# GpSimd's first subtraction behind each norm waits for the diagonal matrices, and TensorE multiplies a block of ones meanwhile

## The reference, cut to what matters

```python
def rmsnorm(x, w):
    x32 = x.astype(jnp.float32)
    y = x32 * lax.rsqrt(jnp.mean(x32 * x32, axis=-1, keepdims=True) + NORM_EPS)
    return (y * w.astype(jnp.float32)).astype(x.dtype)
...
    for i in range(DEPTH):
        h = rmsnorm(x, norm_mix[i])
        x = x + token_mixer(h, w_in[i], ...)
        x = x + peer(rmsnorm(x, norm_ffn[i]), peer_wq[i], peer_keys[i], peer_u[i], peer_v[i])
    return rmsnorm(x, norm_final)
```

## Time and profile before

| | us |
|---|---|
| median of 3 runs | 2109.36 |
| lowest and highest | 2107.76 and 2110.62 |
| the profiled execution, its own time | 2112.14 |
| span of its trace, first to last instruction | 2110.0 |
| granted TensorE clock, mean over the span | 0.984 |

### The profile page before, as it was taken

One profiled execution on the slowest core, in us unless ns is written; L12 is line 12 of the kernel. 1 busy time (PEld: TensorE's weight loads), 2 busy tenths in 40 slices (PEclk: granted clock), 3 DMA queues, 4 the chain that ended last, 5 costly groups with the idle time before them and its releaser, 6 DMA issues.

```text
span 2110.0 us, 40295 instructions
## 1 busy us (share of the span) xinstructions
PE 2021.6 (96%) x13604; PEld 1856.2 (88%) x13604; DVE 1258.7 (60%) x2835; ACT 973.1 (46%) x1431; POOL 1283.8 (61%) x624
## 2 busy tenths in 40 slices
PE   7988999999999999999989879999999999999998
PEld 7787999999999888888787869999999998888886
DVE  6555099538888544444475550994388885444444
ACT  4444454653333454554544434446533334445454
POOL 5334679976666555555463337899766665555553
PEclk9999999999999999999999999999999999999999
DMA  6423455554444555555534225545444445555554
GB/s 208 145 80 100 160 185 167 171 175 140 139 139 139 169 190 196 190 195 193 184 121 151 90 81 174 195 159 175 166 140 140 138 140 176 194 194 191 196 190 139
DMA packets 93242, 338.44 MB, mean 160 GB/s; under 512 B 10353, under 2 KB 10737, under 8 KB 93169
## 3 DMA queue, kind: packets, MB, share of 16 engines
q1 hardware_dynamic: 93168, 337.53, 47.7%
HBM read 336.44 MB, written 1.05 MB: 160 GB/s over the span
## 4 chain that ended last, share of the span: by engine, by line
PE 85%; DVE 7%; POOL 3%; issue 2%; ACT 1%; DMA 1%; POOLq 0%; DVEq 0%; SPq 0%; ACTq 0%
PE PS L885 33%; PE PS L829 10%; PE PS L824 10%; PE PS L825 10%; PE PS L837 5%; PE PS L530 4%; POOL WL L444 3%; DVE G L1382 2%; PE PS L514 2%; PE PS L515 2%; PE PS L750 2%; PE PS L519 2%; PE PS L496 1%; PE PS L625 1%; DVE G L1379 1%
## 5 line engine op out<-in xcount | busy, mean ns | idle before, releaser
L444 POOL TENSOR_TENSOR WL<-ring,WH 128x1024 fp32r<-128x1024 f32 x360 | 910.0, 2533 | 486.1 <-ACT WH L955 244.6
L1119 ACT CAST WH<-ring 128x1024 fp32r<-128x1024 f32 x512 | 538.0, 1051 | 814.1 <-PE PS L825 380.8
L470 POOL TENSOR_TENSOR HL<-G,HH 128x256 fp32r<-128x256 f32 x256 | 372.5, 1455 | 324.4 <-ACT HH L1212 324.3
L1702 DVE TENSOR_TENSOR WL<-ring,WH 128x1024 fp32r<-128x1024 f32 x248 | 303.7, 1225 | 371.0 <-ACT WH L1119 371.0
L824 PE MATMUL PS<-HH,WH 128*128 128x256 f32 x2048 | 512.2, 288 | 0.0
L825 PE MATMUL PS<-HL,WH 128*128 128x256 f32 x2048 | 501.3, 283 | 0.0
L825 PEld LDWEIGHTS PS<-HL,WH 128*128 128x128 f32 x2048 | 392.2, 192 | 0.0
L824 PEld LDWEIGHTS PS<-HH,WH 128*128 128x128 f32 x2048 | 391.8, 191 | 0.0
L885 PE MATMUL PS<-WH,HH 128*128 128x512 f32 x1024 | 315.4, 389 | 3.0 <-issue 3.0
L885 PE MATMUL PS<-WH,HL 128*128 128x512 f32 x1024 | 315.3, 389 | 0.0
L829 PE MATMUL PS<-HH,WL 128*128 128x256 f32 x2048 | 289.1, 284 | 12.4 <-POOL WL L444 12.4
(11 more groups left out here) (237 smaller groups left out, 2306.8 us busy)
## 6 DMA issues: line engine op xcount, KB each, us to landing
ring<-stream SPq DMA_DIRECT2D x636, 512.0 KB, 3.3
X<-x_t SPq DMA_DIRECT2D x4, 256.0 KB, 4.4
out_t<-X SPq DMA_DIRECT2D x2, 512.0 KB, 2.7
CN<-consts SPq DMA_DIRECT2D x1, 843.5 KB, 9.7
WF<-last SPq DMA_DIRECT2D x1, 512.0 KB, 10.2
PR<-params SPq DMA_DIRECT2D x2, 239.0 KB, 4.4
CN<-consts SPq DMA_DIRECT2D x1, 64.0 KB, 5.1
```

The lines of the kernel that those rows point to most:

```text
L444: nc.gpsimd.tensor_tensor(WL[:, b, :], ring[:, slot, :], WH[:, b, :].bitcast(F32), ALU.subtract).then_inc(done, 1)
L470: nc.gpsimd.tensor_tensor(GL[:, s, :], G[:, tile, :], GH[:, s, :].bitcast(F32), ALU.subtract).then_inc(L.gl_ready, 1)
L1119: nc.scalar.copy(WH[:, b, :], ring[:, slot, :]).then_inc(L.hi_ready, 1)
L1702: V.tensor_tensor(WL[:, s % 2, :], ring[:, (U0 + s) % SLOTS, :], WH[:, s % 2, :].bitcast(F32), ALU.subtract).then_inc(L.vlo_ready, 1)
```

## The change

GpSimd gets a wait ahead of two of a layer's subtractions. For q == 0 it waits until the layer's first two diagonal matrices are there, for n == 2 * WQ0 until the next two are. TensorE gets a function `spin` that multiplies `ones` with itself a given number of times, with the result in the first 128 columns of chunk 0's place, and each time on its own (no accumulation). At the head of `h_turn` it runs 11 such products in a layer's first norm and 9 in its second. In layer 0 another 13 run before that, behind a wait for `ones`. The first real product into that place overwrites what they leave.

```diff
@@ gpsimd
                         elif layer > 0:
                             pool.wait_ge(last.piece_done, PIECES - 1 + q)
+                        if q == 0:
+                            pool.wait_ge(L.diag_ready, TT)
+                        if n == 2 * WQ0:
+                            pool.wait_ge(L.diag_ready, 2 * TT)
                         low(q % 2, n % SLOTS, L.mix_lo)
@@ tensor
+                    def spin(o, n):
+                        for _ in range(n):
+                            nc.tensor.matmul(o, ones[:, :], ones[:, :], start=True, stop=True)
+
                     def h_turn(k):
 
+                        spin(h_part(k, 0)[:, 0:P], 9 if k else 11)
                         pe.wait_ge(L.diag_ready, TT * (k + 1))
                         for c in range(DC):
@@ tensor, ahead of the first h_turn of a layer
+                    if layer == 0:
+                        pe.wait_ge(s_ones, 1)
+                        spin(h_part(0, 0)[:, 0:P], 13)
                     h_turn(0)
```

## The result

The change took the kernel from 2109.41 to 2094.76 us, each the median of six runs. The ratio is 0.9921, with a 95% interval of 0.9903 to 0.9939, so the gain lies between 12.9 and 20.5 us. The runs after spread from 2086.89 to 2096.40. The forecast was 2095.0, in a range of 2091.5 to 2101.0. The profiled execution took 2095.60 us (span 2093.5), 16.5 less than that of before; the forecast for it was 14.5 less. In the experiments they shift again by a few lines; the tiles in a row (`ones`; `DG,X`; `HH,WL`; `DG`) name the same work. "Lower product" stands for the first product of L519, by whatever number, behind a norm.

The account below looks back on a forecast made before the run. The prediction took TensorE to bound the kernel, with 85% of the chain that ended last. Gains of 6.2 us (collision) and 8.2 (clock), 14.5 in all, from the median gave 2094.9, stated as 2095.0, range 2091.5 to 2101.0.

Parts of the forecast that it names:

- The wait on GpSimd: At the norms' DG writes: the pair takes 0.48 us and the turn starts 2.08 us sooner in three norms.
- The turn at full clock: In all four norms' turns: with TensorE's clock high throughout, the first L519 product stands 6.0 us behind the turn's start.
- T + 6.0: T is the start of a norm's turn; the first L519 product was to start 6.0 us later, instead of 7.73 to 8.91.
- The ones fit and hold the clock: Ahead of the turns: products of ones end in time, 1.5 to 1.7 us stay idle in later norms, clock stays up.
- Layer 0's first norm, 1.73 us: First L519 product at 16.14 instead of 17.87, a gain of 1.73 us with the ends -1.2 and 1.8.
- 6.2 for the collision: In three norms: 6.2 us in all from DG writes that no longer stand still while GpSimd subtracts.
- 8.2 for the clock: In the norms' turns: 8.2 us of the 14.5 us sum from turns at full clock.
- ones that do not hold the clock: Rival at the turns: the clock falls as now, only the collision's 6.2 us go, 2103.1; chance 9%.
- the second rival: At the DG writes: slow for another reason than GpSimd, only the clock's 8.2 us come, 2101.1; chance 2%.
- more meetings in the convolution: Rival in the mixer: VectorE's convolution meets more subtractions, about 2.2 us each; nine give 2114.7; chance 5%.
- A shift by one meeting: Between VectorE's convolution and subtractions in the mixer: one meeting more or fewer, 2.2 us either way, well possible.
- the clock's fall at 1129.9: In a stretch of transposes and narrow products, TensorE busy 0.98: cited for the rival that ones do not hold the clock.

Follow-up runs that it names:

- second trace: The change itself run again unaltered as a control on another chip, beside the kernels by chunks: 2094.13 us, ratio 0.9917.
- the two versions by chunks: The change with the turn's results handed over by single chunks, 2093.14 us; the same with layer 0's second weight cast moved behind the chunks, 2091.60 us.
- the version with ScalarE's matrices: The change without GpSimd's two waits, with the diagonal matrices written by ScalarE instead of VectorE: 2096.19 us, ratio 0.9928.
- The last kernel: The change with hand-over by single chunks, and layer 0's second weight piece cast by ScalarE behind the eight chunks instead of ahead: 2091.60 us, ratio 0.9910.

## Why the prediction was right

The mechanism was right, and three of its four norms came out to 0.03 us. That the median, 2094.76, lies 0.24 us from the 2095.0 of the forecast is in part luck: the norms of the trace gave 14.0 us and not 14.5, the runs after spread over 9.5 us, and the gain was 14.7 us the first time and 16.8 the second.

**The wait on GpSimd, 2.08 us in three norms: right.** The pairs take 0.48 us. The wait ahead of n == 2 * WQ0 holds the next subtraction with it, and no product waits for the two.

**The turn at full clock, lower product at T + 6.0: right to 0.02 us** in three norms, for the reason given, the pace of ScalarE and VectorE. The gains of 4.99, 3.89 and 3.87 were 4.97, 3.86 and 3.84.

**The ones fit and hold the clock: right.** In the last three norms they ended 1.33 to 1.50 us before the turns, in the first 0.51. The forecast took as its bounds a fall 2.3 us behind a last product and a pause with 1.65 us idle. The runs agree with that: 1.3 to 1.5 us idle kept the clock in the three later turns of the change, of its second trace and of the two versions by chunks, twelve in all; 1.54 to 1.71 us kept it in the three of the version with ScalarE's matrices; 2.45 us kept it once and lost it once, and 2.61 us kept it; and 3.3 to 4.0 us lost it in all six turns traced without one of the two parts.

**Layer 0's first norm, 1.73 us: the term that was mis-sized.** It was 1.37. The step that failed was "T + 6.0" for this norm too: it was T + 6.70, and T + 7.35 in the second trace. Timelines of TensorE and ScalarE, after:

```profile
1.07 8.22 PE L498 MATMUL PS<-ones 128*128 128x128 f32 x48 [1.07 <-DVE ones L1268]
9.80 3.84 PE L507 MATMUL PS<-DG,X 128*128 128x128 f32 x32 [0.51 <-DVE DG L1310]
...
9.69 1.04 ACT L969 CAST WH<-ring 128x1024 fp32r<-128x1024 f32 x1 [1.32 <-DMA ring<-stream]
10.97 1.05 ACT L969 CAST WH<-ring 128x1024 fp32r<-128x1024 f32 x1 [0.23 <-DMA ring<-stream]
11.92 3.03 ACT L1017 ACTIVATE HH<-PS,PR 128x256 fp32r<-128x256 f32 x8
```

The ones end at 9.29, inside the 8.1 to 9.3 that was forecast, and the turn runs at full clock. But ScalarE's two casts wait for their transfers, and it takes the first chunk at T + 2.1 instead of 1.2, right behind the second cast. The lower product stands 4.6 us behind that chunk, and the turn's start hardly matters: in the second trace the turn started 0.76 us sooner (9.04) and the lower product only 0.11 (16.39). A cold turn had hidden that. The last kernel shows it: with one cast moved, this norm also takes 5.59 us from the turn's start. That the granted clock's column reads 1.00 here says nothing, as forecast: the first 13 records of ones took 2.93 us, the pace of half clock, and the later ones 0.11 each.

**What was not seen.** The forecast split the 14.5 us into 6.2 for the collision and 8.2 for the clock, and gave 2103.1 for ones that do not hold the clock. GpSimd's waits alone took 2.08 us or a little more out of each of the three waits, so the 6.2 stands, and their median of 2105.35 is near the price. But the 8.2 us are not the work of the ones: alone they gave nothing. They belong to the two parts together. For the same reason the price of the second rival was wrong, 2101.1 for a write that stays slow: with the write slow, the kernel with the ones took 2110.14. The rivals: the clock was held; the write was stalled by GpSimd. Of more meetings in the convolution there is no sign: its writes' medians are as before (2.27 and 0.49 us), and TensorE's wait for them at the mixer's first transposes is 7.2 us in both traces. A shift by one meeting, which the forecast called well possible, did come in the profiled execution, though at the mixer's end and not in the convolution: it is the 2.7 us above.

One row was misread. The forecast took the clock's fall at 1129.9 as a sign that not all work counts alike. The microsecond of the fall was busy 0.98, but the two before it were busy 0.55 and 0.38, so the row does not show that. Idle time had gone before, and the fall showed up behind it, as in the runs described at the end.

## What to carry to other kernels

Ask of every short write by VectorE on a critical chain which subtraction or other GpSimd work may start beside it, and let that work wait if nobody needs it soon. The same stall still stands late in this kernel's mixers, 3.6 us of TensorE's time when both writes meet a subtraction; no run here moved those subtractions. Filling TensorE's wait with throw-away products pays when what stays idle is short, here 1.3 to 1.7 us; shorten the wait first, then fill it, and stop filling before the data comes, since each product too many costs its full time. When a stage is sped up, look for what the slow version had covered: here two casts that waited for transfers.

## What the runs showed that I had not expected

The same idle time of 2.45 us behind the same work lost TensorE's clock in one norm and kept it in another, in one execution. And in layer 0's second norm the fall came only after TensorE had started again: at 203.7 behind a start at 202.29 with fewer ones, at 209.9 behind 208.75 with the waits alone, at 207.4 behind 207.11 with the ones alone. The idle time had gone by at full clock, and the turn paid for it.

One kernel's executions on one chip differ by more than I had thought: the runs of before span 11.7 us (2103.82 to 2115.49), those with the parts apart 14 to 16, with a mean granted clock from 0.982 to 0.990. In the traces, apart from the norms, these differences sit in the mixers and not in the experts' stages. Two causes are seen there: writes of VectorE that meet a subtraction, and falls of the clock behind short waits.
